# A two-layer trunk with eight experts: the one-hot matrices of experts 1 to 7 built on GpSimd instead of VectorE

## The reference

```python
logits = h @ w_router
top_vals, top_idx = lax.top_k(logits, 2)
gates = softmax(top_vals)
comb = sum(one_hot(top_idx, 8) * gates[..., None])
y = 0
for e in range(8):
    y = y + comb[..., e:e + 1] * ((silu(h @ wg[e]) * (h @ wu[e])) @ w_down[e])
```

## Time and profile before

| | |
|---|---|
| median of 3 runs | 1783.42 us (1782.84 to 1784.57) |
| the profiled execution: time | 1783.2 us |
| its span | 1781.4 us |
| mean granted clock of PE in it | 0.962 of full speed |
| busy: PE, DVE, ACT, POOL | 1637.2, 1267.4, 1021.9, 10.6 us |
| HBM read | 449 MB, 253 GB/s over the span |

### The profile page before, as it was taken

How to read it: one execution, slowest core, us unless ns; L and a number is a source line. 1 busy time by engine, 2 the same in 40 slices (tenths; PEclk the granted TensorE clock), 3 DMA queues, 4 the chain that set the end, 5 groups by cost and what they waited for, 6 DMA issues and landing times.

```text
span 1781.4 us, 20893 instructions
## 1 busy us (share of the span) xinstructions
PE 1637.2 (92%) x7345; PEld 1330.9 (75%) x7346; DVE 1267.4 (71%) x1092; ACT 1021.9 (57%) x872; POOL 10.6 (1%) x26
## 2 busy tenths in 40 slices
PE   7999999999899869999999999899999599898996
PEld 5887778888787657777778878778887477677775
DVE  6745554444588569999988888555554599799796
ACT  4344343443456537878867767544443488687684
POOL 0000000000000000000000000000000000000000
PEclk9999999999999869999999999899999799899998
DMA  9653455555522129999999889656564399899894
GB/s 355 194 189 109 163 177 189 188 188 189 188 97 71 47 76 377 397 365 387 394 345 370 329 322 364 237 185 212 192 217 156 126 382 395 296 386 395 302 394 177
DMA packets 191592, 450.84 MB, mean 253 GB/s; under 512 B 8492, under 2 KB 8892, under 8 KB 191420
## 3 DMA queue, kind: packets, MB, share of 16 engines
q1 hardware_dynamic: 189212, 445.35, 69.8%
q10 hardware_dynamic: 2336, 4.85, 0.7%
HBM read 449.13 MB, written 1.05 MB: 253 GB/s over the span
## 4 chain that ended last, share of the span: by engine, by line
PE 71%; DVE 11%; DMA 8%; ACT 5%; issue 4%; DVEq 0%; SPq 0%; ACTq 0%; POOL 0%; POOLq 0%
PE bank L1140 19%; PE bank L1141 19%; PE bank L1144 19%; DMA raw<-in_moe_w_down 8%; DVE wlo L691 6%; PE bank L1147 4%; ACT whi L396 4%; PE bank L1148 3%; DVE y L929 2%; PE bank L1417 1%; PE bank L1418 1%; PE bank L1315 1%; PE bank L1317 1%; PE bank L1433 1%; PE bank L1434 1%
## 5 line engine op out<-in xcount | busy, mean ns | idle before, releaser
L691 DVE TENSOR_TENSOR wlo<-raw,whi 128x2048 fp32r<-128x2048 f32 x422 | 962.6, 2290 | 323.1 <-ACT whi L396 322.2
L396 ACT ACTIVATE whi<-raw 128x2048 fp32r<-128x2048 f32 x422 | 804.9, 1915 | 457.6 <-PE bank L1144 376.9
L1140 PE MATMUL bank<-whi,xx 128*128 128x512 f32 x1184 | 481.3, 406 | 62.7 <-issue 28.1
L1141 PE MATMUL bank<-wlo,xx 128*128 128x512 f32 x1184 | 473.2, 400 | 0.0
L1144 PE MATMUL bank<-whi,xx 128*128 128x512 f32 x1184 | 473.0, 400 | 0.0
L1140 PEld LDWEIGHTS bank<-whi,xx 128*128 128x128 f32 x1184 | 230.2, 194 | 114.5 <-issue 35.9
L1144 PEld LDWEIGHTS bank<-whi,xx 128*128 128x128 f32 x1184 | 229.3, 194 | 49.8
L1141 PEld LDWEIGHTS bank<-wlo,xx 128*128 128x128 f32 x1184 | 230.2, 194 | 46.7
L1147 PE MATMUL bank<-whi,hT 128*128 128x512 f32 x336 | 138.8, 413 | 23.7 <-DVE wlo L691 22.5
L1147 PE MATMUL bank<-whi,xx 128*128 128x512 f32 x336 | 133.3, 397 | 0.2 <-DVE wlo L691 0.2
L1148 PE MATMUL bank<-wlo,hT 128*128 128x512 f32 x336 | 132.3, 394 | 0.0
(11 more groups left out here) (200 smaller groups left out, 1246.0 us busy)
## 6 DMA issues: line engine op xcount, KB each, us to landing
raw<-in_moe_w_gu SPq DMA_DIRECT2D x224, 1024.0 KB, 7.6
raw<-in_moe_w_down SPq DMA_DIRECT2D x112, 1024.0 KB, 7.8
raw<-in_ffn_w_gu SPq DMA_DIRECT2D x28, 1024.0 KB, 5.1
raw<-in_ret_w_in SPq DMA_DIRECT2D x24, 1024.0 KB, 6.6
raw<-in_ffn_w_down SPq DMA_DIRECT2D x14, 1024.0 KB, 4.8
raw<-in_conv_w_pw SPq DMA_DIRECT2D x12, 1024.0 KB, 5.1
raw<-in_ret_w_out SPq DMA_DIRECT2D x8, 1024.0 KB, 4.9
res<-in_x SPq DMA_DIRECT2D x2, 512.0 KB, 4.9
```

Of the source, the lines that this page charges most:

```text
L396: nc.scalar.activation(whi[base % SPLIT][:, :], raw[base % RAW][:, :], ACT.Copy).then_inc(hi_done, 1)
L691: nc.vector.tensor_tensor(wlo[base % SPLIT][:, :], raw[base % RAW][:, :], whi[base % SPLIT][:, :].bitcast(f32), ALU.subtract).then_inc(lo_ ...
L1140: nc.tensor.matmul(dst, ah, bh, start=start, stop=False)
L1141: last = nc.tensor.matmul(dst, ah, bl, start=False, stop=stop and al is None)
```

## The change

It removes the wait and the build from `expert` on DVE and puts both on POOL, in a Python loop that is unrolled, so that the places of `slot` are constants. POOL first waits for DVE's build of expert 0, then before each of the eight builds for PE's transposition of the matrix that it overwrites. Its semaphore counts and the data are those of before.

```diff
@@ gpsimd
             root(3)
+
+            pool.wait_ge(onehot_done, 1)
+            for e in range(NE):
+                pool.wait_ge(ohT_ps, e + 1)
+                for h in range(2):
+                    for n in range(2 * TILES):
+                        at_ = n % 2 * P + h * HALF
+                        last = nc.gpsimd.tensor_scalar(onehot[:, n // 2, at_:at_ + HALF], iota[:, h * HALF:(h + 1) * HALF],
+                                                       slot[:, e + 1, n, h:h + 1], None, ALU.is_equal)
+                last.then_inc(onehot_done, 1)
             root(4)
@@ vector, expert(e, tiles)
                 hidden(done, B_MOE + 4 + 6 * six, tiles)
-                dve.wait_ge(ohT_ps, e + 1)
-                build_onehot(e + 1)
                 lo(B_MOE + 4, six)
                 lo(B_MOE + 5, six)
```

## The result

| | before | changed |
|---|---|---|
| median of 4 runs | 1783.13 us (1782.75 to 1784.57) | 1758.74 us (1751.77 to 1762.88) |
| ratio to before, 95% interval | | 0.9858, 0.9830 to 0.9886 |
| the profiled execution: span | 1781.4 us | 1750.0 us |
| mean granted clock in it | 0.962 | 0.970 |

The kernel is 24.4 us faster; I had forecast 11.8, and a range that ended at 1762. The direction was right and the size off by a factor of two. In two more sets of runs the changed kernel measured 1763.3 (ratio 0.9859 to 0.9901) and 1764.0 (0.9872 to 0.9911). Against the runs of before that stand beside them, 1782.8 and 1783.4, these two gain 19.5 and 19.4 us.

What follows compares the result with a forecast made beforehand. PE was taken as the bound, waiting behind DVE's build at each expert, with DMA limiting half-tile experts. Build -10.3, clock -2.8, POOL's interference +1.0 gave -12.1 us on 1783.2, plus 0.2 for the median: 1771.3, range 1762 to 1780.

Steps and rivals of the forecast that it cites:

- The build leaves DVE, eight times: At each expert's first block, `lo` and PE start 1.29 us earlier without the build on DVE: 10.3 us saved.
- Does it survive to the end?: Half-tile experts keep the 1.29 us because `lo` frees the first buffer earlier and the DMA stream shifts as much.
- a hole in the DMA stream: DMA engines run dry at an expert's boundary: 1.7 us at expert 1, 3.6 at expert 2, both over 1.29.
- The clock: Behind PE's shortened gaps the clock stays at 1.00: 1.4 us each in experts 2 and 3, zero in half-tile experts.
- The rival that had the clock count everywhere: Clock gain of 1.4 us counts in seven experts, half-tile ones included: 20.1 us saved, 1763.1 us; chance 0.08.
- 23 times, 12.4 us: ACT's copies wait this often and long for blocks to land, all in half-tile experts; taken as DMA bound there.
- one gap of 1.82 us: PE's gap in two-tile expert 4, after which the clock stayed at 1.00; the shorter remaining gaps should do likewise.
- The build arrives on POOL: Each compare takes 0.25 us on POOL, eight 2.0, at most 4.4; hidden within 97 us before the gather.
- What POOL does to DVE: POOL's compares beside `hidden` and `lo` delay DVE by half a POOL instruction per expert: 1.0 us lost.
- the slower rival: POOL takes the port for the whole build, `lo` waits for all eight compares: 1788 to 1804 us; chance 0.12.

Runs made afterwards that it cites:

- The idle compares: Changed kernel plus eight compares per expert on DVE at the build's old place, into a tile nobody reads: 1784.41 us, ratio 1.0012.
- the clock's experiment: Kernel before, build still on DVE, plus 8 (two-tile expert: 6) matmuls of zeros in PE's gap behind its transposes: 1773.31 us, ratio 0.9940.
- the run with four compares: Changed kernel plus four compares per expert on DVE at the build's old place, into a tile nobody reads: 1777.31 us, ratio 0.9956.
- 24 compares: Changed kernel plus 16 more compares on GpSimd in front of each build, into a tile nobody reads: 1763.34 us, ratio 0.9888.

## Why the prediction was wrong, step by step

- **"The build leaves DVE, eight times", 10.3 us: right.** The gaps shrank from 2.34, 2.84 and 1.82 to 1.04, 1.54 and 0.55 us, 1.29 each. Expert 4, where nothing else changed, gained 1.28. The idle compares gave it all back.
- **"Does it survive to the end?": right in the result, wrong in the reasoning.** I let the gain through a hole in the DMA stream that was just long enough. The first step became as short in the profile in which that hole closed as in the one in which it stayed, and the clock's experiment shortened it without moving the stream's start. The stream was not the limit of the first step.
- **"The clock": this step failed.** That it would stay up was right in all seven places. Two things were wrong. The size was 1.4 us and measured 1.6; seven matmuls in 3.0 us were counted between two rows, and the lower level lasted 3.4. And above all I gave it zero in the half-tile experts: "PE would be done sooner and then wait for the stream". They gained the same 1.6 us as the others, 5 x 1.63 = 8.2 us that the sum lacked. The clock's experiment shows it without moving the stream's start. With all seven at their measured size my sum would have been -10.3 - 11.4 + 0, and 0.2 to the median, so 1761.7, against 1762.5 for the median of the changed kernel's 14 runs. The rival that had the clock count everywhere said 1763.1 and got a chance of 0.08.
- **Where that error came from.** I read "23 times, 12.4 us" as blocks that pin the kernel. None of the waits is longer than 0.8 us, and the later steps of the half-tile experts take 15.1 to 15.7 us beside them. My reading, which no run tests by itself, is that ACT waits there for a landing in time that it would else have spent waiting for PE. In the changed kernel such waits rose to 17.0 and once to 25.1 us, with at most 1.7 us more for the five later steps of an expert in its three profiles. And the DMA engines were not at full load in the stretch that holds the gap; they come near it in the next three microseconds, as the share in the last column but one shows, of before and, three us wide as well, of the changed kernel:

```profile
664.50:667.50 3.00, 1.72 (x5) 1.36 (x6) 3.00 (x2) 1.37 (x1) 0.00 (x0) 0.79 0.15 16
667.50:670.50 3.00, 3.00 (x11) 2.36 (x10) 3.00 (x3) 0.04 (x1) 0.00 (x0) 0.64 0.94 346
```

```profile
663.40:666.40 3.00, 3.00 (x13) 2.51 (x14) 3.00 (x3) 1.36 (x1) 3.00 (x3) 1.00 0.58 168
666.40:669.40 3.00, 3.00 (x15) 2.46 (x15) 2.95 (x2) 2.19 (x2) 3.00 (x2) 1.00 1.02 395
```

  The share of 1.03 that I cited the earlier trace rows is of the later steps. That does not make the DMA bound a phantom: it is close behind. From the first `hidden` of expert 1 to that of expert 2 the shares of before and of the changed kernel are

```profile
777.16:894.31 117.15, 109.91 (x502) 87.12 (x502) 109.04 (x73) 90.88 (x63) 0.00 (x0) 0.99 1.02 381
```

```profile
773.07:887.91 114.84, 108.64 (x502) 85.80 (x502) 108.01 (x64) 91.13 (x64) 13.16 (x8) 1.00 1.04 391
```

  so the stream is now at full load over this whole expert, and its five later steps took 76.23 us where they had taken 75.69. How much further such an expert could be shortened beside the stream, no run here settles.
- **The evidence for the clock was thinner than I wrote.** I argued from one gap of 1.82 us after which it stayed up. In the run with four compares, a gap of 1.80 let it fall, one of 1.85 did not, and three of 1.85 did; with `lo` in front of `hidden`, one of 1.82 let it fall. The gaps that the change leaves, 0.54 to 1.54 us, did not let it fall at any of the 24 places in the changed kernel's three profiles; but in the run with the build moved on DVE it fell once, after 1.54 us in expert 2. My forecast of the clock was right with luck in its grounds.
- **"The build arrives on POOL": hidden, as said, but not at that price.** I took 0.25 us for a compare and 4.4 for eight at most. One alone takes 0.44, and beside `lo` it waits for it. POOL in the changed kernel and in expert 4 alone, where `lo` is rare, least, median and greatest in ns:

```profile
L375 POOL TENSOR_SCALAR onehot<-mats,slot x64: 437/2350/4652, 660.6 to 1643.5; 128x64 fp32r<-128x64 f32 x64
...
L375 POOL TENSOR_SCALAR onehot<-mats,slot x8: 441/444/2598, 1163.7 to 1172.7; 128x64 fp32r<-128x64 f32 x8
```

Eight take 13.2 to 15.4 us in a single-tile expert. The cover of 97 us made the error harmless.
- **"What POOL does to DVE", +1.0 us: nothing measurable.** `lo` was 2279/2292/2296 ns before and is 2274/2293/2361 now; its mean rose by 2 ns, 0.7 us over all 335 in the experts. The Trainium skill's "SBUF — State Buffer", section "Who interferes with whom", says that such a pair excludes each other and that the second blocks until the first is done. The trace agrees for GpSimd, of whose 64 compares 38 took about one or two lengths of `lo`, and the rest 0.44 to 0.46 us. For DVE it does not: a `lo` that met a compare in flight would be up to 0.44 us late, and the greatest is 0.07 over the rest, 0.09 with 24 compares. One such meeting is in expert 2 of the changed kernel: the `lo` that starts at 898.56 found a compare 0.11 us old, the compare ended after 0.44 all the same, and the `lo` took 2.345. So the slower rival, 0.12 of the chances, had its mechanism in the chip but with the roles turned round.
- **The range.** Its end at 1762 came from that one rival alone. The first set, at 1758.7, is also the fastest of the three; the others, 1763.3 and 1764.0, lie just inside the range. So 4 to 5 us of the miss are the draw of that set, and the nearly 8 us that the forecast misses by in every set are the clock's term. With 5 us more at its end for the scatter of the changed kernel (1751.8 to 1768.3), which the three tight runs of before did not show, the range would have reached 1757.

## What to carry to other kernels

A gap of PE that ends with the lower clock costs itself and the slow stretch behind it, here 1.29 us of another engine's time against 2.9 us of gain; so look at the granted clock behind each gap, and price the two parts apart. A few matmuls of zeros in the gap give the second part without touching the first. A list of short waits for a DMA does not show that the stream sets the length: here the experts with 23 of them gained as much in the changed step as those with none. Before calling a stream the bound, look at its share in the stretch behind the change, and not only in the steady part.

## What the runs showed of the hardware that I had not expected

- A GpSimd compare of 128 x 64 takes 0.44 us alone and 2.35 or 4.65 beside DVE's subtractions of two SBUF inputs (2.29 us each), while these keep their length: DVE goes first. Eight such compares took up to 15.4 us of POOL's time and nothing measurable of DVE's.
- DVE's own short compares are the ones that lose a little: 239 to 346 ns beside POOL's, 245 to 254 alone.
- Nearly equal gaps of PE, 1.80 and 1.85 us, at the same place of two equal experts left the clock at different levels for the next three us; of four gaps of 1.85 in that execution, three let it fall. At this place it stayed up after 1.93 us in another run (expert 4, eight idle compares); after gaps of 2.25 us and more it always fell, and three times, behind gaps of 2.25, 2.35 and 3.17 us, it stayed down for 6.8 us instead of 3.4.
- PE stands idle for 3.3 to 20.7 us at four of seven expert boundaries under "issue"; in one execution of the changed kernel one of the four was absent and it was the fastest of all. The profiles show transfers of the instruction queue, 16 KB each, around these places, and 32 of them instead of 34 in that execution; the two that are missing are those that the other profiles have at this boundary. That PE waits there for its program is likely, but no run here tests it.
